# A hybrid decoder layer on one core: order of the stage before the experts, and a triangular inverse with crossed heads

## The reference, cut to what matters

```python
h = rms_norm(x, norm1) * (1 + scale1(c)) + shift1(c)
q, k, v, p_rw, g_a, g_b = split(h @ w_in)
o_a = window attention(q, k, v), with a sink per head:
    p = softmax(concat([s, sink]))[..., :-1]
for each token t of a head:                      # RWKV-7, state S is 64 x 64
    sa = S @ (-kk_t)
    S = S * w_t + sa * (kk_t * a_t) + v_t * k_t
    o_t = S @ r_t
m = sigmoid(g_a) * (o_a @ w_pa) + sigmoid(g_b) * (group_norm(o) @ w_pb)
x = x + gate1(c) * (m @ w_o)
x = x + gate2(c) * moe(h2)                       # top 4 of 32 experts, D 1024, hidden 1024
```

## Time and profile before

| | us |
|---|---|
| median of 3 runs (1312.58 to 1316.66) | 1313.81 |
| the profiled execution | 1313.82 |
| its span, first to last instruction | 1312.0 |
| TensorE busy (96% of the span) | 1255.2 |
| VectorE busy (34%) | 451.5 |
| ScalarE busy (23%) | 301.9 |
| GpSimd busy (4%) | 52.8 |
| mean granted TensorE clock, of full speed | 0.991 |

### The profile page before, as it was taken

How to read it: one execution, slowest core, us unless ns; L and a number is a source line. 1 busy time by engine, 2 the same in 40 slices (tenths; PEclk the granted TensorE clock), 3 DMA queues, 4 the chain that set the end, 5 groups by cost and what they waited for, 6 DMA issues and landing times.

```text
span 1312.0 us, 21013 instructions
## 1 busy us (share of the span) xinstructions
PE 1255.2 (96%) x8339; PEld 626.3 (48%) x8339; DVE 451.5 (34%) x1035; ACT 301.9 (23%) x554; POOL 52.8 (4%) x66
## 2 busy tenths in 40 slices
PE   7998997989999999999999999999999999999997
PEld 5787776878753333333333333333333333333333
DVE  2145648436343322223322222332222233222225
ACT  3012441121132212112212112222211222212112
POOL 0000531300000000000000000000000000000000
PEclk9999998999999999999999999999999999999999
DMA  9966341236689999999999999999999999999993
GB/s 366 359 243 246 114 160 43 63 134 261 257 311 404 426 425 430 427 430 428 428 430 427 429 428 428 430 428 429 428 428 430 427 429 428 428 430 427 429 428 146
DMA packets 55606, 467.05 MB, mean 356 GB/s; under 512 B 5141, under 2 KB 7449, under 8 KB 29690
## 3 DMA queue, kind: packets, MB, share of 16 engines
q1 hardware_dynamic: 53354, 461.07, 84.7%
q0 software_dynamic: 1664, 5.20, 1.4%
q10 hardware_dynamic: 544, 0.13, 0.0%
HBM read 463.91 MB, written 5.09 MB: 357 GB/s over the span
## 4 chain that ended last, share of the span: by engine, by line
PE 75%; DMA 18%; DVE 3%; ACT 2%; issue 1%; SPq 0%; DVEq 0%
PE ps L1361 26%; DMA ring<-in_w 15%; PE ps L1388 14%; PE ps L1305 6%; PE ps L865 5%; PE ps L1330 4%; DMA ring<-in_w_in 3%; PE ps L1250 2%; PE ps L1218 2%; PE ps L855 2%; PE ps L1369 2%; PE ps L1312 1%; PE ps L874 1%; ACT PT L751 1%; PE ps L1118 1%
## 5 line engine op out<-in xcount | busy, mean ns | idle before, releaser
L1361 PE MATMUL ps<-ring,PT 128*64 128x512 f32 x1536 | 337.3, 593 | 7.8 <-DMA ring<-in_w 7.6
L1822 DVE TENSOR_TENSOR SQ<-ps,SQ 128x528 f32<-128x528 f32 x128 | 81.6, 699 | 609.3 <-PE ps L1330 609.3
L1361 PEld LDWEIGHTS ps<-ring,PT 128*64 128x64 f32 x1536 | 109.7, 137 | 229.3 <-issue 210.3
L1388 PE MATMUL ps<-ring,PT 128*64 128x512 f32 x768 | 170.1, 595 | 0.0
L746 ACT COPY HT<-ps 128x512 f32<-128x512 f32 x64 | 34.4, 589 | 392.2 <-PE ps L1361 392.2
L1361 PE MATMUL ps<-arena,PT 128*64 128x512 f32 x512 | 113.2, 593 | 2.6 <-DMA arena<-in_w 2.6
L1388 PEld LDWEIGHTS ps<-ring,PT 128*64 128x64 f32 x768 | 53.2, 137 | 99.8 <-issue 99.8
L1305 PE MATMUL ps<-XR,PT 128*64 128x512 f32 (+1 forms) x396 | 97.1, 607 | 0.1
L1330 PE MATMUL ps<-PT 64*128 64x264 f32 x512 | 74.0, 408 | 0.0
L1361 PEld LDWEIGHTS ps<-arena,PT 128*64 128x64 f32 x512 | 36.6, 137 | 76.5 <-issue 70.4
L865 PE MATMUL ps<-HT,ring 128*128 128x264 f32 x304 | 71.0, 394 | 0.0
(11 more groups left out here) (432 smaller groups left out, 1157.3 us busy)
## 6 DMA issues: line engine op xcount, KB each, us to landing
ring<-in_w SPq DMA_DIRECT2D x144, 2048.0 KB, 27.0
arena<-in_w SPq DMA_DIRECT2D x48, 2048.0 KB, 27.5
ring<-in_w_mod SPq DMA_DIRECT2D x12, 2048.0 KB, 14.3
ring<-in_w_in SPq DMA_DIRECT2D x9, 2048.0 KB, 14.6
ring<-in_w_o SPq DMA_DIRECT2D x2, 2048.0 KB, 11.4
ring<-in_w_pa SPq DMA_DIRECT2D x1, 2048.0 KB, 9.1
ring<-in_w_pb SPq DMA_DIRECT2D x1, 2048.0 KB, 8.9
bias_rows<-bias_by_distance POOLq DMA_DIRECT2D x1, 1536.0 KB, 14.3
```

The lines of the kernel that those rows point to most:

```text
L1361: last = mm(ps[64 * lin:64 * lin + 64, 2 + hh, :], XG[:, k % 4, k // 4, :], slot_tile(slot, c)[:, k % 2, lin * FE + hh * 512:lin * FE + hh ...
L1388: last = mm(ps[64 * hh:64 * hh + 64, 4, :], AC[:, f, :], slot_tile(slot, c)[:, f % 4, hh * 512:hh * 512 + 512], start=(f == 0), stop=(f == ...
L1822: v.tensor_tensor(YA[:, p::4, :], ps[:, bank:bank + 2, 0:T], YA[:, p::4, :], ALU.add).then_inc(sem["comb_used"], 1)
```

## The change

- The transposes of values and the key rows move in front of the low rank products, into banks 5 to 7; decay and rate products stand ahead of the first eight gate steps, the output gate's behind them. ScalarE loads the exponential's table by a one-element operation, makes the decays' exponentials before the gate's copies; VectorE makes the scans before it scales NK.
- The sink is written as one more column of the score tile, so that maximum, exponential and sum take it in; the division by the sum is four `tensor_scalar` instead of one `tensor_tensor`.
- The gate steps are spread differently: 8, 12, 12, 16, 16, 1, 12, 3, 10, 4, 2, 4, 4 instead of 8, 12, 20, 12, 12, 1, 12, 3, 8, 3, 4, 4, 5 x 1.
- In the sample group, VectorE's copies for the attention stand ahead of large products of the recurrence, semaphores are merged, and the sample output (two products and two reductions by halves), SOE and the bonus move from before the masks into the levels 1 to 4 and behind them.
- Level 0 and the first mask go by halves n. From level 0 on every second pair of heads (`other`) keeps Y and XX in the other half of the partitions than X: Y, the X update, U0 and XZW of these heads read one half and write the other, the XX update reads and writes the same half. The order `quads` alternates four quarters. X and XX have semaphores of their own.
- A block of projections (L865) and small router products are moved in front of the wait for the output's additions, and of the group norm's sums.

```diff
+            def level_mask(i, units):
                 mask = cst[:, K_LV + 64 * i:K_LV + 64 * i + 64].unsqueeze(1).broadcast_to([P, 16, CH])
-                pool.tensor_tensor(NM[i % 2], NR[:, :, 0:CH], mask, ALU.mult).then_inc(sem["nm_ready"], 1)
+                pool.tensor_tensor(NM[i % 2][:, units, :], NR[:, units, 0:CH], mask[:, units, :], ALU.mult).then_inc(sem["nm_ready"], 1)
+
+            for n in range(2):
+                pool.wait_ge(sem["xs_ready"], n + 1)
+                level_mask(1, slice(8 * n, 8 * n + 8))
+            for i in range(2, len(LEVELS)):
+                pool.wait_ge(sem["y_done"], 2 * i - 2)
+                if i == 2:
+                    pool.wait_ge(sem["xs_ready"], 2)
+                level_mask(i, slice(0, 16))
...
+            act.wait_ge(sem["kvrow_done"], 1)
+            act.copy(vr[:, 0:2, :], ps[:, 5, 0:2 * P].rearrange("p (a b) -> p a b", b=P))
+            act.copy(vr[0:NS, 2, :], ps[0:NS, 5, 2 * P:3 * P])
+            act.wait_ge(sem["kvrow_done"], 3)
+            act.copy(kd, ps[:, 6:8, 0:T])
+            act.copy(kvr[:, 0, :], ps[:, 6, T:T + P])
+            act.copy(kvr[0:NS, 1, :], ps[0:NS, 7, T:T + P]).then_inc(sem["kvrow_evac"], 1)
+            act.activation(warm, epsc[0:1, 0:1], ACT.Exp)
+            act.wait_ge(sem["cs_ready"], 1)
+            act.activation(eP, CS, ACT.Exp).then_inc(sem["decays"], 1)
+            act.activation(eN, CS, ACT.Exp, scale=-1.0).then_inc(sem["decays"], 1)
+            act.activation(dec[:, :, :], LD[:, :, NP:T], ACT.Exp).then_inc(sem["decays"], 1)
+            gates(0)
...
-                    act.activation(Pm[:, g, 0:J], Pm[:, g, 0:J], ACT.Exp, bias=st[:, 4 + g:5 + g],
+                    act.activation(Pm[:, g, 0:J + 1], Pm[:, g, 0:J + 1], ACT.Exp, bias=st[:, 4 + g:5 + g],
                                    accum_out=st[:, 8 + g:9 + g]).then_inc(sem["att_exp"], 1)
-                act.activation(st[:, 12:16], st[:, 12:16], ACT.Exp).then_inc(sem["att_exp"], 1)
...
+                    act.copy(by_group(Y[:, 8 * n:8 * n + 8, :]),
+                             ps[:, 4 * n:4 * n + 2, 0:256].rearrange("p s (g k) -> p s g k", g=2)).then_inc(sem["y_evac"], 1)
...
-            gates(8)
+            pe.wait_ge(sem["qk_ready"], 1)
+            for n, (t0, nt) in enumerate(TILES):
+                last = tr(ps[0:nt, 5, n * P:n * P + P], PTv[:, CV, t0:t0 + nt], ID)
+            last.then_inc(sem["kvrow_done"], 1)
+            for kv, (t0, nt) in enumerate(TILES[1:]):
+                pe.wait_ge(sem["sh_evac"], 3 + kv)
+                mm(ps[:, 6 + kv, 0:T], II[64 * kv:64 * kv + 64, :], PTv[64 * kv:64 * kv + 64, CK, :], start=True, stop=True)
+                tr(ps[0:nt, 6 + kv, T:T + P], PTv[:, CK, t0:t0 + nt], ID).then_inc(sem["kvrow_done"], 1)
...
+            gates(8)
...
             scores(0)
+            gates(12)
             pe.wait_ge(sem["qs_evac"], 1)
             scores(1)
-            gates(20)
+            gates(12)
             probabilities(0)
             scores(2)
             values(0)
-            gates(12)
+            gates(16)
             probabilities(1)
             scores(3)
             values(1)
-            gates(12)
+            gates(16)
             probabilities(2)
...
+            def other(h, par):
+
+                return 1 - par if h // 2 % 2 else par
...
-            pe.wait_ge(sem["row_evac"], 8)
-            gates(8)
-            pe.wait_ge(sem["smp_att"], 3)
+            pe.wait_ge(sem["smp_att"], 4)
...
-            gates(3)
+            pe.wait_ge(sem["row_evac"], 8)
+            gates(10)
...
+            quads = [(h + d, par) for h in (0, 1, 4, 5) for d in (0, 2) for par in range(2)]
+
+            def in_group(h):
+
+                return 2 * (h // 4) + h % 2
+
+            def group_out(to, n, h, lo):
+
+                col = lo + in_group(h) * CH
+                return ps[64 * to:64 * to + 64, 4 * n + h // 2 % 2, col:col + CH]
...
+            for n in range(2):
+                pe.wait_ge(sem["nm0_ready"], n + 1)
+                pe.wait_ge(sem["nr_ready"], n + 1)
+                pe.wait_ge(sem["kr_ready"], n + 1)
+                for h, par in quads:
+                    u, q = 8 * n + h, other(h, par)
+                    if q != par:
+                        col = in_group(h) * CH
+                        mm(ps[64 * q:64 * q + 64, 4 * n + 2, col:col + CH], II[64 * par:64 * par + 64, 0:CH], half(NM[0], par)[:, u, :],
+                           start=True, stop=True)
+                    last = mm(ps[64 * par:64 * par + 64, 4 * n, h * CH:h * CH + CH], half(NM[0], par)[:, u, :], II[64 * par:64 * par + 64, 0:CH],
+                              start=True, stop=True)
+                last.then_inc(sem["y_done"], 1)
+            for i in range(1, len(LEVELS)):
...
+                    pe.wait_ge(sem["nm_ready"], n + 1 if i == 1 else i + 1)
+                    pe.wait_ge(sem["x_ready"], 2 * (i - 1) + n + 1)
+                    for h, par in quads:
+                        u, q = 8 * n + h, other(h, par)
+                        last = mm(group_out(q, n, h, 0), half(NM[i % 2], par)[:, u, :], half(X, par)[:, u, :], start=True, stop=True)
...
                     pe.wait_ge(sem["y_evac"], 2 * (i - 1) + n + 1)
+                    pe.wait_ge(sem["xx_ready"], 2 * (i - 1) + n + 1)
                     if i < len(LEVELS) - 1:
-                        for _, h, par in units[:16]:
-                            u = 8 * n + h
-                            last = mm(ps[64 * par:64 * par + 64, 4 * n + 1, h * CH:h * CH + CH], half(XX, par)[:, u, :],
-                                      half(Y, par)[:, u, :], start=True, stop=True)
-                    for _, h, par in units[:16]:
-                        u = 8 * n + h
-                        last = mm(ps[64 * par:64 * par + 64, 4 * n + 2, h * CH:h * CH + CH], half(Y, par)[:, u, :],
-                                  half(XX, par)[:, u, :], start=True, stop=True)
+                        for h, par in quads:
+                            u, q = 8 * n + h, other(h, par)
+                            last = mm(group_out(par, n, h, 256), half(XX, q)[:, u, :], half(Y, q)[:, u, :], start=True, stop=True)
+                        last.then_inc(sem["d_done"], 1)
+                    for h, par in quads:
+                        u, q = 8 * n + h, other(h, par)
+                        last = mm(ps[64 * q:64 * q + 64, 4 * n + 2, h * CH:h * CH + CH], half(Y, q)[:, u, :],
+                                  half(XX, q)[:, u, :], start=True, stop=True)
                     last.then_inc(sem["dx_done"], 1)
...
+                gates(4)
...
+            project([8], range(1, 2))
             pe.wait_ge(sem["carry_evac"], 5)
             pe.wait_ge(sem["ot_ready"], 1)
             pe.wait_ge(sem["soe_ready"], 1)
             mm(ps[:, 5, 0:32], SOE, cst[:, K_SL:K_SL + 32], start=True, stop=True).then_inc(sem["smp_o"], 1)
-            project([8], range(1, 2))
-            pe.wait_ge(sem["smp_step"], 2)
-            for hp in range(4):
-                mm(ps[:, 4 + hp, 0:T], BO, OT[:, hp, :], start=True, stop=True).then_inc(sem["gn_done"], 1)
...
+            def sinks(g4):
+
+                J = P if g4 < 2 else 2 * P
+                chain(v.tensor_copy(Pm[:, :, J:J + 1], sinkb[:, 4 * (g4 % 2):4 * (g4 % 2) + 4].unsqueeze(2)))
...
-                chain(v.tensor_reduce(st[:, 0:4], Pm[:, :, 0:J], AX.X, ALU.max))
-                chain(v.tensor_tensor(st[:, 0:4], st[:, 0:4], sinkb[:, heads], ALU.max))
-                chain(v.tensor_scalar(st[:, 4:8], st[:, 0:4], -1.0, None, ALU.mult))
-                done(v.tensor_tensor(st[:, 12:16], sinkb[:, heads], st[:, 4:8], ALU.add), "att_max", g4 + 1)
+                chain(v.tensor_reduce(st[:, 0:4], Pm[:, :, 0:J + 1], AX.X, ALU.max))
+                done(v.tensor_scalar(st[:, 4:8], st[:, 0:4], -1.0, None, ALU.mult), "att_max", g4 + 1)
                 if g4:
                     att_out(g4 - 1)
-                dve.wait_ge(sem["att_exp"], 5 * g4 + 5)
-                chain(v.tensor_tensor(st[:, 8:12], st[:, 8:12], st[:, 12:16], ALU.add))
+                dve.wait_ge(sem["att_exp"], 4 * g4 + 4)
                 chain(v.reciprocal(st[:, 8:12], st[:, 8:12]))
-                done(v.tensor_tensor(Pm[:, :, 0:J], Pm[:, :, 0:J], st[:, 8:12].unsqueeze(2).broadcast_to([P, 4, J]), ALU.mult),
-                     "att_p", g4 + 1)
+                for g in range(4):
+                    ins = v.tensor_scalar(Pm[:, g, 0:J], Pm[:, g, 0:J], st[:, 8 + g:9 + g], None, ALU.mult)
+                    if g == 3:
+                        done(ins, "att_p", g4 + 1)
...
+            chain(v.tensor_reduce(sa[:, 0:16], T1[:, 0:16, :], AX.X, ALU.add))
             dve.wait_ge(sem["smp_done"], 2)
             chain(v.tensor_copy(pTs, ps[:, 5, 0:64]))
-            done(v.tensor_copy(PSf, ps[0:NS, 5, 64:128]), "smp_att", 2)
+            done(v.tensor_copy(PSf, ps[0:NS, 5, 64:128]), "smp_att", 3)
```

(30 more changed lines are left out.)

212 lines of the change are left out of this document (92 added, 120 removed).

## The result

The changed kernel takes 1300.82 us, median of 4 runs (1299.22 to 1302.22), where the kernel before, measured beside it, took 1314.0. The ratio is 0.9896 [0.9881, 0.9911]: 1.0% faster, 13.2 us, half of the 26.6 forecast, and just above the range's end of 1299. The mixers start at 287.45 instead of 302.29, where 275.7 was forecast.

A forecast was written before the change was run, and what follows sets the result against it. The prediction took TensorE to be the bound ahead of the mixers, whose start the expert loop hangs on. Gains of 2.2 + 5.1 + 15.0 + 4.3 = 26.6 us took 1313.81 to 1287.2 us, range 1280 to 1299.

The forecast's parts named there:

- part 3: Masks and inverse, first score product to carry products: 36.5 us instead of 51.5, VectorE the bound, 15.0 us gained.
- Part 2: Sample stage up to the first score product: TensorE's gap of 2.93 us goes and the OS copy comes earlier, 5.1 us gained.
- Part 1: Key rows, low rank products and softmax, 126 to 187 us: 2.2 us gained, bounds 4 gained to 2 lost.
- Part 4: Carry to mixers: eight gate steps fill the idle 2.53 us and run at full clock, 5.33 to 3.56; 4.3 us gained.
- Rival A: Inverse levels: the clock falls, batches double, 7.7 us a level against 4.2; costs 17 us, total 1304; chance 0.09.
- Rival B: Softmax: the division by row, now four instructions, may stall; its sign is four divisions each 2 us long; chance 0.14.
- Rival C: Inverse: crossing gives nothing, 9.5 us less gain, total 1297; chance 0.05.
- Rival D: Inverse: crossed products hold one another up and run one at a time, 1.87 us a batch; 33 us, total 1320; chance 0.03.

The follow-up runs named there:

- e12: Changed kernel with 36 extra crossed batches of 16 products issued without a wait ahead of level 1: 1334.59 us, ratio 1.0155.
- e5: Changed kernel with level products for every second head only, 128 columns instead of two times 64, Y scaled by zero (inverse left out): 1292.86 us, ratio 0.9825.
- e4: Changed kernel with eight of the ten gate steps put back ahead of the sample output's transposing product: 1297.66 us, ratio 0.9880.
- e11: Changed kernel with the eight gate steps put back behind the wait for the output's additions: 1303.99 us, ratio 0.9917.
- e8: Changed kernel measured and profiled again with nothing altered: 1301.06 us, ratio 0.9895.
- e2: Changed kernel with eight gate steps moved from behind XZW into levels 1 to 4: 1299.65 us, ratio 0.9894.
- e10: Changed kernel with six more products of a gate step's size, without effect, in front of the mixers' first: 1302.29 us, ratio 0.9918.
- e1: Changed kernel with the crossing alone undone, every head's products reading and writing the same half of the rows: 1303.85 us, ratio 0.9922.
- e6: Changed kernel with 12 crossed, 12 uncrossed and 12 crossed 128-column batches issued without a wait ahead of level 1: 1331.0 us, ratio 1.0125.
- e3: Changed kernel with 32 of 64 columns in the level products, Y scaled by zero (inverse left out): 1305.51 us, ratio 0.9931.

## Why the prediction failed, step by step

The failed step is part 3: "So the bound changes to VectorE, 4.2 us a level with its waits." Measured 5.5 a level, and 46.1 us for 36.5 from the first score product to the carry. The rate of a crossed product was read rightly (0.5 us for 16, and 128 records in 1.9 us in e12), but from bursts: the 32 carry products of the earlier trace rows are 128 instructions, a stock that is already there. Six batches a level are not a burst. The term that the forecast put at nothing is the supply of instructions: 384 a level at 256 in 3.74 us. With the instructions halved (e5) the same stage takes 37.4 us and a level 4.16: the count of VectorE's work was right, and 8.7 of the 9.6 missing us went with the instructions. Most of the 0.9 that are left stand ahead of the levels: the masks written down behind 5.7 (2 x 1.24, 0.7 and 0.5 us) don't add up to 8.4, and both halves of X were ready at 10.5, not 9.9. By place, changed kernel against e5: 1.6 us up to the first X addition of the levels, 3.7 in the three periods behind it, 3.4 from there to the carry. What could have warned was in the profile before: uncrossed batches of 0.93 us in the levels with no idle piece, beside an instruction queue that ran a 16 KB piece every 4.2 us. With TensorE busy throughout, nothing showed that the supply had hardly room above that rate.

Part 2: 2.9 for 5.1. The OS copy came at 202.47 (forecast 202.3), TensorE idled 2.53 (2.85), the clock fell as said. Its price was put at 1.6 us; the ten steps took 8.05 us for 4.45, 0.57 of it a wait for ScalarE's copy of a gate block, so the low clock cost 3.0:

```profile
201.80:208.50 6.70, 5.75 (x16) 4.55 (x17) 6.13 (x8) 0.00 (x0) 0.00 (x0) 0.50 0.00 1
```

Behind 284.05 it was low for about 3 us and behind 202.16 for 10; here for 6.8, between the two, and the forecast took the shorter one. The term was mis-sized by 2 us with the wait. e4 shows the larger miss: with the idle piece filled, both the wait and the low clock go.

Part 1: 1.3 for 2.2, inside its bounds; the waits behind the output gate's products came (0.87 and 0.60 us), and the granted clock was 0.50 from 140.4 to 143.7, where a gate step took 0.88 us, so that twelve took 7.25 instead of 5.3. That is the fall that the bounds priced at 1.8. Part 4: 4.4 for 4.3; e11 shows both of its terms.

Rival A (the clock falls in the levels): not in the first profile, 1.00 over the stage. In the second (e8) it fell in the last level, behind the longest stop:

```profile
247.10:250.50 3.40, 3.40 (x101) 3.35 (x98) 2.07 (x3) 1.17 (x2) 0.00 (x0) 0.50 0.00 0
```

The same fall stands in e2, e10 and e11; the stage took 46.8 us in e8 instead of 46.1, so it costs about 1 us and not 17. Rival B is there, in the slack. VectorE and GpSimd, changed kernel, and below them the same divisions of a later group:

```profile
147.62 4.69 DVE L1614 TENSOR_SCALAR ring<-ring,st 128x128 f32<-128x128 f32 x4
152.35 2.22 DVE L1584 COPY ring<-sinkb 128x4 f32<-128x4 f32 x1
...
149.63 2.41 POOL L457 TENSOR_TENSOR PT<-ring 128x1024 f32<-128x1024 f32 x1
152.12 2.42 POOL L458 TENSOR_TENSOR PT<-arena,ring 128x1024 f32<-128x1024 f32 x1
...
168.89 1.14 DVE L1614 TENSOR_SCALAR ring<-ring,st 128x256 f32<-128x256 f32 x4
```

Four small divisions take 4.7 us beside GpSimd's products, and four of twice the size 1.1 us where GpSimd has nothing to do; TensorE has no idle time from 147.6 to 156, so nothing of it reached the path. No run undid them alone. Rival C came nearer to the measured time (1297) than the forecast, by the wrong mechanism: crossing gives 4.4 us of the 9.5 (e1), and does speed single batches. Rival D (crossed products one at a time, 1.87 us a batch): no, 0.47 between the stops.

Left open: why a piece of 256 instructions takes 3.5 to 4.0 us when its transfer takes 0.9 to 1.4; and whether fewer instructions could be had in the levels with the right result, since e5 leaves heads out.

## What to carry to other kernels

Before small products are sped up, count their instructions, weight loads and all, against the rate at which the trace shows the instruction queue refill: a batch that runs fast once may not run fast six times. When TensorE stops with "issue" at equal counts of records, put long products there, which need few instructions (e2), or use wider ones (e5). Put filler ahead of a wait, not behind it, since the idle piece also costs the clock for the steps that follow.

## What the runs showed of the hardware

- TensorE's instructions came at 256 per 3.74 us in a quiet stretch (e12, DMA share 0.02); beside transfers (share 0.96) one load came 6.25 us after the one before. Between two stops crossed products of 64 columns went at twice that rate (128 records and their weight loads in 1.9 us).
- Uncrossed products of 64 by 64 run at 0.93 to 0.97 us for 16, nearly the same rate: 12 batches took 11.6 us, crossed 11.5 (e6). Uncrossed they ran there without a stop; whether the array or the supply holds them, no run tells.
- With products of 32 columns the granted clock fell to 0.50 behind a stop of 1.55 us and stayed there from 227.4 to 258.1, although TensorE was recorded busy 30.68 of these 30.70 us (e3; the ends of its products are modelled).
- The same code with the same idle piece of 1.2 us kept the clock in one execution (e8) and in the other had 0.62 of it over 8 us (the first profile).
- Four divisions of 128x128 on VectorE took 4.69 us beside GpSimd's products of 2.4 us; four of 128x256 took 1.14 us where GpSimd was idle.
